# Normalising between the stages of a three-block network: row sums with one-column matmuls and a spread, or already spread sums from a block of ones

## The chip, the cores and the metric

The kernel runs on one core of one Trainium2 chip. The metric is the device time of one execution in microseconds (us), lower is better. Three runs of the kernel before gave a median of 3197.14 us (3194.56 to 3199.7).

## The reference

The input is 256 tokens of 1024 features, float32. Three blocks of layers follow each other: feed-forward layers, a hybrid of a short convolution and attention, sparse attention, attention with forget gates, a convolution module with a LayerNorm, a mixture of eight experts, a pooled and block attention, a cross-attention and a convolved feed-forward layer. Almost every layer begins with the same step, a normalisation of each token by its own root mean square:

```python
def rms_norm(x, g):
    xf = x.astype(jnp.float32)
    y = xf * lax.rsqrt(jnp.mean(xf * xf, axis=-1, keepdims=True) + EPS)
    return (y * g.astype(jnp.float32)).astype(x.dtype)

def modulate(x, g, shift, scale):
    return rms_norm(x, g) * (1 + scale[:, None]) + shift[:, None]
```

The convolution module has a LayerNorm over 768 features: subtract the mean, divide by the root of the variance plus EPS, times a gain, plus an offset.

## The kernel before

The activations lie turned: features on the partitions, tokens along the free dimension. `X` is eight tiles of 128 features by 256 tokens; `T` is scratch of the same shape. A norm therefore has to sum over partitions and tiles, and its result, one number for each token, is needed on every partition. Each weight matrix comes in chunks of 128x2048 floats into `ring`; ScalarE rounds a chunk to `whi` (line 1869), VectorE takes the rest as `wlo` (line 2792), and TensorE multiplies with three matmuls for each product (`mm3`, line 541): upper by upper, upper by lower, lower by upper. `hh` and `hl` are the same two parts of the normalised activations.

Each engine has a class (`Pe`, `Act`, `Dve`, `Pool`, `Sp`) that writes its own program in order; engines meet only at semaphores, by `wait_ge`. What an engine does around a norm is thus set by the order in which its class writes it.

A stage ends with a down projection (`down_steps`, line 767): output tiles j = 0 to 7, two of them to a bank of PSUM. After each pair VectorE adds the result to `X` (`finish`, line 2925, two instructions for a pair), ScalarE squares the new tiles into `T` (`squares`, line 1899: 0 and 1, 2 and 3, 4 and 5 as one instruction of 512 columns each, 6 and 7 alone), and TensorE sums the squares (`stat_part`, line 597). The table `NEXT` (line 519) says which norm follows which stage. In the last step of the stage TensorE puts the sums of tiles 0 and 1 behind output tile 5, those of 2 and 3 behind tile 6, and those of 4 to 7 behind tile 7. A sum is a matmul whose stationary operand is half a tile of squares (128 tokens) and whose moving operand is one column of ones, so a tile takes two, and the result has tokens on partitions, 128x2.

The tail of a norm then runs: `root` (line 1912) takes the square root of the 128x2 on ScalarE into `st`, `rinv` (line 2807) the reciprocal on VectorE, `spread` (line 622) brings it to all partitions with two matmuls against the identity, 128x256 in PSUM, and `scale` (line 2833) multiplies every tile of `X` by its gain and by that. ScalarE copies each tile to `hh`, VectorE subtracts for `hl`, and the first matmuls of the next stage start when `hl` of tile 0 is there. TensorE meanwhile runs `heat(6)` (line 646), twelve matmuls on a constant tile whose result nobody reads.

Nine norms come from `NEXT`: `hy`, three of feed-forward layers of block 1, `nsa`, `n_ffn2`, `cv`, `moe` and `n_ffn3`; a tenth entry, `final`, has sums of its own. The norm `moba` follows the experts, and its eight tiles are summed in one go by `stat` (line 590). In the convolution layer (`conv_layer`, lines 1405 and 3582) the mean goes the same way (`spread("mean")`), then VectorE subtracts it, and the norm `cvln` sums six tiles of squares. Some norms inside the attention stages already take another way: `wide_sum` (line 614) with a stationary block of ones or pairs, `wide_root` (line 1925) and `wide_inv` (line 3398) over the whole spread tile; `mem3` is one of these.

In the prediction an "instruction pair" of TensorE is a load of weights and its matmul; a float32 matmul of the program is two such pairs.

## Time and profile before

| | |
|---|---|
| median of 3 runs | 3197.14 us |
| the profiled execution | 3200.52 us |
| its span, first to last instruction | 3198.4 us |
| TensorE (PE) busy | 3072.9 us, 96% |
| VectorE (DVE) busy | 2305.3 us, 72% |
| ScalarE (ACT) busy | 1698.1 us, 53% |
| mean granted TensorE clock | 0.967 of full |

The busy shares are averages over stages with different limits. The page also has a chain of waits: from the last instruction back, at each step to what released it. A timeline lists the instructions of one engine in order of time, equal neighbours merged; PEld is TensorE's loading of weights, PE its matmuls.

### The profile page before, as it was taken

Reading aid. Unit: us, or ns where it says so; the run is one execution under the profiler, and the core shown is the slowest. Engines: PE = TensorE matmul, PEld = TensorE weight load, DVE = VectorE, ACT = ScalarE, POOL = GpSimd, SP = SyncE. Lnnn points to the kernel's source line nnn. Section 1 sums busy time; section 2 is a strip of 40 time slices with the busy share of each in tenths; the row PEclk is TensorE's granted clock in tenths of the full one; section 3 lists DMA queues with packets and bytes.
Section 4 is the critical chain, followed back from the end, with each engine's and each line's share of the span. In section 5 each row is a group of like instructions: output and inputs, shape, how many; then the busy total and the mean of one; then the engine's idle time right before and its main releaser. Section 6 shows DMA issues by size and latency. Waiting matters only on the chain.

```text
span 3198.4 us, 48532 instructions
## 1 busy us (share of the span) xinstructions
PE 3072.9 (96%) x20796; PEld 2821.9 (88%) x20796; DVE 2305.3 (72%) x2588; ACT 1698.1 (53%) x1905; POOL 84.1 (3%) x163
## 2 busy tenths in 40 slices
PE   8999899999988999899979999999999999999999
PEld 6999799999988998899968888888888888899999
DVE  5786668788555556654585898898898888666575
ACT  4434343443534435443535777777777777545453
POOL 1010001011000000000000000000000000000000
PEclk8999999999989999999988999999999999999999
DMA  7785458678421653235412999999899899533353
GB/s 284 261 324 192 158 185 302 230 293 307 159 73 67 221 207 132 80 145 185 171 41 99 367 352 343 361 355 362 340 353 356 342 357 365 201 119 132 118 187 118
DMA packets 112317, 739.27 MB, mean 231 GB/s; under 512 B 12481, under 2 KB 12481, under 8 KB 32097
## 3 DMA queue, kind: packets, MB, share of 16 engines
q1 hardware_dynamic: 89424, 651.21, 54.3%
q0 software_dynamic: 22672, 84.91, 7.4%
q8 instruction: 166, 2.72, 0.3%
q14 instruction: 55, 0.44, 0.0%
HBM read 735.01 MB, written 1.05 MB: 230 GB/s over the span
## 4 chain that ended last, share of the span: by engine, by line
PE 77%; DVE 7%; ACT 3%; issue 1%; DMA 1%; DVEq 0%; ACTq 0%
PE ps L539 57%; PE ps L538 18%; PE ps L548 2%; DVE wlo L2792 2%; DVE AF L2771 2%; ACT whi L1869 1%; DMA ring<-in_w 1%; DVE att L2780 0%; DVE gf L2774 0%; DVE hl L2762 0%; DVE AF L2762 0%; ACT cv L1854 0%; DVE gs L2777 0%; DVE T L2762 0%; ACT L1854 0%
## 5 line engine op out<-in xcount | busy, mean ns | idle before, releaser
L2792 DVE TENSOR_TENSOR wlo<-ring,whi 128x2048 fp32r<-128x2048 f32 x620 | 1417.1, 2290 | 451.7 <-ACT whi L1869 450.7
L1869 ACT ACTIVATE whi<-ring 128x2048 fp32r<-128x2048 f32 x620 | 1185.3, 1914 | 365.5 <-issue 200.6
L539 PE MATMUL ps<-whi,AR 128*128 128x512 f32 (+1 forms) x2884 | 912.7, 392 | 3.1 <-DVE wlo L2792 2.8
L539 PE MATMUL ps<-hh,whi 128*128 128x256 f32 x2464 | 696.0, 282 | 3.6 <-DVE wlo L2792 3.2
L539 PE MATMUL ps<-hh,wlo 128*128 128x256 f32 x2464 | 688.5, 279 | 0.0
L539 PE MATMUL ps<-hl,whi 128*128 128x256 f32 x2464 | 688.3, 279 | 0.0
L539 PEld LDWEIGHTS ps<-whi,AR 128*128 128x128 f32 x2884 | 537.2, 188 | 119.0 <-DVE wlo L2792 3.5
L539 PE MATMUL ps<-wlo,AR 128*128 128x512 f32 (+1 forms) x1442 | 558.5, 387 | 0.0
L539 PEld LDWEIGHTS ps<-hh,whi 128*128 128x128 f32 x2464 | 462.8, 188 | 8.9 <-DVE wlo L2792 3.4
L539 PEld LDWEIGHTS ps<-hl,whi 128*128 128x128 f32 x2464 | 462.9, 188 | 1.2 <-issue 1.0
L539 PEld LDWEIGHTS ps<-hh,wlo 128*128 128x128 f32 x2464 | 462.5, 188 | 0.3
L538 PE MATMUL ps<-AR,whi 128*128 128x256 f32 x2112 | 380.8, 282 | 0.0
L538 PEld LDWEIGHTS ps<-AR,whi 128*128 128x128 f32 x2112 | 324.9, 189 | 0.0
L539 PEld LDWEIGHTS ps<-wlo,AR 128*128 128x128 f32 x1442 | 272.2, 189 | 58.9
L538 PE MATMUL ps<-AR,wlo 128*128 128x256 f32 x1056 | 296.8, 281 | 0.0
L1854 ACT ACTIVATE gs<-ps 128x256 f32<-128x256 f32 (+1 forms) x167 | 75.7, 453 | 274.2 <-PE ps L539 250.2
L538 PE MATMUL ps<-hh,whi 128*128 128x256 f32 x656 | 196.3, 299 | 10.3 <-DVE hl L2762 6.4
L538 PEld LDWEIGHTS ps<-AR,wlo 128*128 128x128 f32 x1056 | 199.7, 189 | 0.0
L538 PE MATMUL ps<-hl,whi 128*128 128x256 f32 x656 | 191.3, 292 | 0.0
L538 PE MATMUL ps<-hh,wlo 128*128 128x256 f32 x656 | 190.9, 291 | 0.0
L1854 ACT ACTIVATE cv<-ps,att 128x256 f32<-128x256 f32 (+1 forms) x144 | 60.5, 425 | 206.4 <-DVE att L2780 206.3
L1854 ACT ACTIVATE AR<-gf 128x512 fp32r<-128x512 f32 x66 | 41.7, 632 | 239.1 <-DVE gf L2762 239.1
(247 smaller groups left out, 3267.8 us busy)
## 6 DMA issues: line engine op xcount, KB each, us to landing
ring<-in_w SPq DMA_DIRECT2D x620, 1024.0 KB, 5.0
rring<-in_r POOLq DMA_DIRECT2D x135, 512.0 KB, 4.8
first<-in_r POOLq DMA_DIRECT2D x16, 512.0 KB, 15.1
AF<-in_mem POOLq DMA_DIRECT2D x2, 1024.0 KB, 7.6
X<-in_x POOLq DMA_DIRECT2D x1, 1024.0 KB, 15.1
AF<-in_cst POOLq DMA_DIRECT2D x1, 1024.0 KB, 5.4
y_out<-X SPq DMA_DIRECT2D x1, 1024.0 KB, 3.9
cst<-in_cst POOLq DMA_DIRECT2D x1, 672.5 KB, 16.3
```

The costliest lines, as they stand in the source:

```text
L538: return self.e.matmul(out, l, r, start=start, stop=stop, skip_group_check=True)
L539: return self.e.matmul(out, l, r, start=start, stop=stop)
L548: return self.e.transpose(out, in_, self.N.ident[0:n, 0:n])
L1854: self.e.activation(out, in_, f, **kw).then_inc(*self.up(*keys))
L1869: self.e.activation(N.whi[:, c % HB, :], N.ring[:, c % RING, :], ACT.Copy).then_inc(N.sem["hi"], 1)
L2771: self.e.scalar_tensor_tensor(out=out, in0=a, scalar=s, in1=b, op0=op0, op1=op1).then_inc(*self.up(*keys))
L2792: self.e.tensor_tensor(N.wlo[:, c % HB, :], N.ring[:, c % RING, :], N.whi[:, c % HB, :].bitcast(F32), ALU.subtract).then_inc(N.sem["lo"], 1)
```

## The change

For the nine norms of `NEXT` other than `final`, for `moba` and for `cvln`, the stationary operand becomes the block of ones (128x128) and the moving operand a whole tile of squares (256 columns), so the sum of a token stands on all partitions at once. ScalarE takes the root of the 128x256 into `xbc`, VectorE its reciprocal in place, and `scale` reads `xbc`; `spread`, `root` and `rinv` go. TensorE's `heat` stands right behind the sums and has 16 matmuls where it had 12 (`moe`, which had none, gets 12). In the nine, VectorE first adds the squares of tiles 0 to 3 (`four_squares`, three instructions written between output tiles 5 and 6 in `finish`), and TensorE has no sums between the output tiles: it sums the added tile and tiles 4 to 7, behind tile 7. The mean of the convolution layer is summed with the block of ones too, and VectorE subtracts it straight from the sums by a scalar_tensor_tensor.

```diff
+WIDE = set(NEXT.values()) - {"final"} | {"moba", "cvln"}
...
     def stat_part(self, key, tiles, part, inds=None):
         n, b = len(tiles), self.ps((key, "ss"))
         for k in part:
             self.wait_ge("act", (key, "sq", k))
+            if key in WIDE:
+                i = self.mm(b[:, 0:S], self.N.ones[:, :], tiles[k], k == 0, k == n - 1)
+                continue
             for tb in range(2):
...
     def norm(self, key, X, which, n=8, T=None):
         T = self.N.T if T is None else T
-        if key not in self.row:
+        if key not in self.summed:
             self.stat(key, [T[:, k, :] for k in range(n)])
-        self.spread(key)
-        self.heat(6)
+        self.w4 += 1
+        self.heat(8)
         self.fresh = key
...
             if f == nf - 1 and key in NEXT:
                 if j == 5:
-                    self.take_row(NEXT[key])
-                    self.take((NEXT[key], "ss"))
-                    self.stat_part(NEXT[key], tiles, (0, 1))
-                elif j == 6:
-                    self.stat_part(NEXT[key], tiles, (2, 3))
+                    self.sum_place(NEXT[key])
+                if NEXT[key] == "final" and j in (5, 6):
+                    self.stat_part(NEXT[key], tiles, (2 * j - 10, 2 * j - 9))
             if j in cuts:
                 yield
         self.chunk_done()
         if f == nf - 1 and key in NEXT:
+            if NEXT[key] != "final":
+                self.wait_ge("dve", (NEXT[key], "four"))
+                self.stat_part(NEXT[key], tiles, (0,))
             self.stat_part(NEXT[key], tiles, range(4, 8))
...
-        self.take_row("mean")
         b = self.take(("mean", "ss"))
         for k, j in enumerate(CONV_ORDER):
             self.wait_ge(*(("dve", ("cv", "conv", j)) if j < 4 else ("act", ("cv", "conv", j))))
-            for tb in range(2):
-                t = self.mm(b[:, tb:tb + 1], N.c_acc[:, j, tb * P:(tb + 1) * P], N.ones[:, 0:1], k == 0 and tb == 0, k == 5,
-                            skip=True)
+            t = self.mm(b[:, 0:S], N.ones[:, :], N.c_acc[:, j, :], k == 0, k == 5)
         t.then_inc(*self.up(("mean", "ss")))
-        self.spread("mean", ready=("act", "sqrt"))
+        self.w4 += 1
...
         self.stat("cvln", [N.T[:, j, :] for j in range(6)])
-        self.spread("cvln")
-        self.heat(6)
+        self.w4 += 1
+        self.heat(8)
...
-        self.spread("moe")
+        self.heat(6)
...
         self.squares(key, X, n, ready or self.ready_x, T)
-        self.root(key, n * P)
+        self.wide_root(key, n * P, N.xbc[:, :])
...
     def norm(self, key, X, which, n=8):
-        self.rinv(key)
+        self.wide_inv(key, self.N.xbc[:, :])
         self.scale(key, X, which, n)
...
+            if j == 5 and NEXT.get(key, "final") != "final":
+                self.four_squares(NEXT[key])
+
+    def four_squares(self, key):
+
+        T = self.N.T
+        for k in (0, 2):
+            self.wait_ge("act", (key, "sq", k + 1))
+            self.tt(T[:, k, :], T[:, k, :], T[:, k + 1, :], ALU.add)
+        self.wait_ge("dve", self.here())
+        self.tt(T[:, 0, :], T[:, 0, :], T[:, 2, :], ALU.add, (key, "four"))
...
-            self.tt(N.c_acc[:, j, :], N.c_acc[:, j, :], b, ALU.subtract, ("cv", "d", j),
-                    *([("free", ("mean", "bc"))] if j == 5 else []))
-        self.rinv("cvln")
-        self.wait_ge("mm", ("cvln", "bc"))
-        b = self.ps(("cvln", "bc"))[:, 0:S]
+            self.stt(N.c_acc[:, j, :], b, -1.0 / 768, N.c_acc[:, j, :], ALU.mult, ALU.add, ("cv", "d", j),
+                     *([("free", ("mean", "ss"))] if j == 5 else []))
+        self.wide_inv("cvln", N.xbc[:, :])
+        self.wait_ge("dve", ("cvln", "inv"))
+        b = N.xbc[:, :]
...
-        self.rinv("moe")
-        self.scaled_rows("moe", N.T, N.X, N.V("norm_ffn_2", 1), 8, lambda k: ("moe", "z", k))
+        self.wide_inv("moe", N.xbc[:, :])
+        self.wait_ge("dve", ("moe", "inv"))
+        for k in range(8):
+            self.stt(N.T[:, k, :], N.X[:, k, :], N.V("norm_ffn_2", 1)[:, k:k + 1], N.xbc[:, :], ALU.mult, ALU.mult,
+                     ("moe", "z", k))
```

## Rows read from the trace of the kernel before

**Rows 1.** The page, part 4: the chain that ended last, by engine.
```profile
PE 77%; DVE 7%; ACT 3%; issue 1%; DMA 1%; DVEq 0%; ACTq 0%
```

**Rows 2.** Timeline, TensorE's weight loads, 611 to 622: start, us, engine, line, count.
```profile
611.98 0.97 PEld L538 LDWEIGHTS ps<-ones,T 128*128 128x128 f32 x8
...
618.90 2.54 PEld L539 LDWEIGHTS ps<-warm 128*128 128x128 f32 x12
621.37 0.19 PEld L538 LDWEIGHTS ps<-hh,whi 128*128 128x128 f32 x1
```

**Rows 3.** Timeline, VectorE, the same norm, 612 to 621.
```profile
612.25 0.88 DVE L2771 SCALAR_TENSOR_TENSOR X<-ps,mod,X 128x256 f32<-128x256 f32 x2 [0.57 <-PE ps L538]
...
619.36 1.26 DVE L2771 SCALAR_TENSOR_TENSOR T<-X,gain,ps 128x256 f32<-128x256 f32 x3 [1.32 <-PE ps L539]
620.54 0.48 DVE L2771 SCALAR_TENSOR_TENSOR hl<-T,mod,hh 128x256 fp32r<-128x256 f32 x1
```

**Rows 4.** Timeline, ScalarE, the same norm: the root.
```profile
617.58 0.26 ACT L1854 ACTIVATE st<-ps,cst 128x2 f32<-128x2 f32 x1 [0.75 <-PE ps L538]
```

**Rows 5.** Timelines of TensorE's loads, ScalarE, VectorE, 2849 to 2858: the norm mem3.
```profile
2849.90 3.32 PEld L539 LDWEIGHTS ps<-AF,ones 128*128 128x128 f32 x16
...
2853.67 0.47 ACT L1854 ACTIVATE xbc<-ps,cst 128x256 f32<-128x256 f32 x1 [2.86 <-PE ps L539]
...
2854.24 1.75 DVE L2777 RECIPROCAL xbc<-xbc 128x256 f32<-128x256 f32 x1 [2.71 <-ACT xbc L1854]
2856.05 2.29 DVE L2792 TENSOR_TENSOR wlo<-ring,whi 128x2048 fp32r<-128x2048 f32 x1
```

**Rows 6.** Timelines, VectorE: the norms hy and of the last feed-forward layer of block 1.
```profile
272.85 0.88 DVE L2771 SCALAR_TENSOR_TENSOR X<-ps,mod,X 128x256 f32<-128x256 f32 x2 [0.55 <-PE ps L538]
...
279.55 0.87 DVE L2771 SCALAR_TENSOR_TENSOR T<-X,gain,ps 128x256 f32<-128x256 f32 x2 [0.81 <-PE ps L539]
...
1009.21 0.87 DVE L2771 SCALAR_TENSOR_TENSOR X<-ps,mod,X 128x256 f32<-128x256 f32 x2 [0.54 <-PE ps L538]
...
1016.76 0.87 DVE L2771 SCALAR_TENSOR_TENSOR T<-X,gain,ps 128x256 f32<-128x256 f32 x2 [1.32 <-PE ps L539]
```

**Rows 7.** Timeline, TensorE's weight loads and VectorE, 405 to 421: after the hybrid stage.
```profile
409.30 1.53 PEld L538 LDWEIGHTS ps<-ones,T 128*128 128x128 f32 x8 [1.89 <-ACT T L1854]
...
407.66 2.44 DVE L2771 SCALAR_TENSOR_TENSOR X<-ps,mod,X 128x256 f32<-128x256 f32 x6
...
420.41 1.26 DVE L2771 SCALAR_TENSOR_TENSOR T<-X,gain,ps 128x256 f32<-128x256 f32 x3 [1.32 <-PE ps L539]
```

**Rows 8.** Timeline, VectorE: the norm n_ffn3.
```profile
2993.58 2.07 DVE L2762 TENSOR_TENSOR X<-X,ps 128x256 f32<-128x256 f32 x6
...
3004.91 0.87 DVE L2771 SCALAR_TENSOR_TENSOR T<-X,sm,ps 128x256 f32<-128x256 f32 x2 [1.32 <-PE ps L539]
```

**Rows 9.** Timelines, TensorE's weight loads and VectorE, 2744 to 2758: the norm moba.
```profile
2747.36 6.59 PEld L538 LDWEIGHTS ps<-ones,T 128*128 128x128 f32 x32 [3.22 <-issue]
...
2755.98 1.26 DVE L2771 SCALAR_TENSOR_TENSOR T<-X,sm,ps 128x256 f32<-128x256 f32 x3 [1.37 <-PE ps L539]
```

**Rows 10.** Timeline, TensorE's weight loads, 1673 to 1677: the mean, the next product.
```profile
1673.09 2.75 PEld L538 LDWEIGHTS ps<-ones,AF 128*128 128x128 f32 x24 [1.65 <-DVE hl L2762]
...
1676.99 0.33 PEld L538 LDWEIGHTS ps<-hh,whi 128*128 128x128 f32 x1
```

**Rows 11.** Busy time by stretch: us, PE, PEld, DVE, ACT, POOL, clock, DMA share, GB/s.
```profile
965.00:966.60 1.60, 0.00 (x0) 0.00 (x0) 1.60 (x3) 0.00 (x0) 0.00 (x0) 1.00 0.00 0
966.70:968.70 2.00, 2.00 (x16) 1.84 (x17) 0.98 (x3) 0.91 (x4) 0.00 (x0) 1.00 0.43 176
1018.90:1020.50 1.60, 1.60 (x9) 1.60 (x9) 1.60 (x5) 1.04 (x3) 0.00 (x0) 0.50 0.00 0
1301.20:1303.50 2.30, 0.00 (x0) 0.00 (x0) 2.30 (x4) 0.00 (x0) 0.00 (x0) 1.00 0.23 96
1304.00:1307.20 3.20, 3.20 (x15) 2.96 (x15) 1.65 (x5) 1.19 (x5) 0.00 (x0) 0.50 0.00 0
```

More of the change, by code:

```diff
@@ L418, in __init__ @@
         self.row, self.rt, self.base, self.span = {}, {}, 4, 4
+        self.summed = set()
         self.sq, self.sqs = 0, []
@@ L592, in stat, with sum_place @@
         n = len(tiles)
-        self.take_row(key)
+        self.sum_place(key)
+        self.stat_part(key, tiles, range(n), inds)
+    def sum_place(self, key):
+        self.summed.add(key)
+        if key not in WIDE:
+            self.take_row(key)
         self.take((key, "ss"))
-        self.stat_part(key, tiles, range(n), inds)
     def stat_part(self, key, tiles, part, inds=None):
@@ L2472, in conv_layer @@
         self.to_T("cvT", 2, "cvo", 6)
-        self.root("mean", 768, func=ACT.Copy)
         self.wait_ge("mm", "cv_mean")
         self.squares("cvln", N.c_acc, 6, lambda k: self.wait_ge("dve", ("cv", "d", k)), N.T)
-        self.root("cvln", 768)
+        self.wide_root("cvln", 768, N.xbc[:, :])
         for j in range(6):
@@ L2490, in moe @@
         self.wait_ge("act", f)
-        self.root("moe", 1024)
+        self.wide_root("moe", 1024, N.xbc[:, :])
         self.raws += 1
@@ L2837, in scale @@
             self.wait_ge("dve", ("part", which[1], 3 * which[2] + 1))
-        self.wait_ge("mm", (key, "bc"))
-        b = self.ps((key, "bc"))[:, 0:S]
+        if key in WIDE:
+            self.wait_ge("dve", (key, "inv"))
+            b = N.xbc[:, :]
+        else:
+            self.wait_ge("mm", (key, "bc"))
+            b = self.ps((key, "bc"))[:, 0:S]
         for k in range(n + 2):
@@ L2842, in scale @@
                 self.stt(N.T[:, k, :], X[:, k, :], gain[:, k:k + 1], b, ALU.mult, ALU.mult, (key, "n", k),
-                         *([("free", (key, "bc"))] if k == n - 1 else []))
+                         *([("free", (key, "bc"))] if k == n - 1 and key not in WIDE else []))
             if k >= 2:
@@ L3650, in conv_layer @@
         self.to_T("cvT", 2, "cvo", 6)
-        self.take_row("mean")
-        self.wait_ge("mm", ("mean", "bc"))
-        b = self.ps(("mean", "bc"))[:, 0:S]
+        self.wait_ge("mm", ("mean", "ss"))
+        b = self.ps(("mean", "ss"))[:, 0:S]
         for j in range(6):
             self.wait_ge(*(("dve", ("cv", "conv", j)) if j < 4 else ("act", ("cv", "conv", j))))
-            self.tt(N.c_acc[:, j, :], N.c_acc[:, j, :], b, ALU.subtract, ("cv", "d", j),
-                    *([("free", ("mean", "bc"))] if j == 5 else []))
-        self.rinv("cvln")
-        self.wait_ge("mm", ("cvln", "bc"))
-        b = self.ps(("cvln", "bc"))[:, 0:S]
+            self.stt(N.c_acc[:, j, :], b, -1.0 / 768, N.c_acc[:, j, :], ALU.mult, ALU.add, ("cv", "d", j),
+                     *([("free", ("mean", "ss"))] if j == 5 else []))
+        self.wide_inv("cvln", N.xbc[:, :])
+        self.wait_ge("dve", ("cvln", "inv"))
+        b = N.xbc[:, :]
         for j in range(8):
@@ L3664, in conv_layer @@
                 self.stt(N.c_acc[:, j, :], N.c_acc[:, j, :], N.V("conv_ln_g_2", 0)[:, j:j + 1], b, ALU.mult, ALU.mult,
-                         ("cvln", "n", j), *([("free", ("cvln", "bc"))] if j == 5 else []))
+                         ("cvln", "n", j))
             if j >= 2:
```

## The prediction

> **What bounds the kernel.** The chain of waits comes first: 77% of it is TensorE [rows 1], so a gain has to be time in which TensorE neither stands nor does avoidable work. Then the timelines around the norms, engine by engine, between the end of one stage and the first product of the next, because there the engines wait for each other in turn and nothing else covers the wait. In one such norm VectorE updates tiles 4 and 5 of `X` at 612.25 and starts scaling at 619.36, and the next stage's first product is loaded at 621.37 [rows 2, 3]. I count each norm from "tile 5 done" (612.25 + 0.88 = 613.13), which the change doesn't touch, to "scaling starts": 6.2 us here. The weight splits for the next chunks are done ahead, so an earlier start of scaling is an earlier stage, whatever bounds the stage later.
>
> **The sum on TensorE.** Before, eight instruction pairs of one column take 0.97 us, 0.12 us each, almost all of it weight loading [rows 2]. Sixteen of them stand between output tiles 5, 6 and 7 and sixteen behind tile 7. The change takes the first sixteen out: 1.9 us at full clock. Behind tile 7 it has five float32 matmuls of 256 columns, ten pairs. The nearest row is exact: in `mem3` sixteen such pairs begin at 2849.90 and occupy 3.32 us, the root starts at 2853.67 [rows 5]. So a pair is about 0.21 us (3.32 less one load of 0.19, over 15), and ten pairs lead from the first load to the root in 3.77 - 6 x 0.21 = 2.5 us.
>
> **The adds on VectorE.** Three tensor_tensor of 128x256 float32. Six such in a row take 2.07 us [rows 8]: 0.42 alone, 0.33 apart. The squares they need come off ScalarE pair by pair behind the updates, and in the timelines those of tiles 2 and 3 end before tile 5 is updated, or within 0.1 us of it. They start at 613.05, 613.39 and, because the third waits for the second, 613.85, and end at 614.27. Queued behind them are the updates of tiles 6 and 7, whose product without the sums is ready about 1.4 us after tile 5's: they start 0.6 us later than they could, but still earlier than now. Their squares are ready before TensorE reaches them. So the sums start at 614.3, 1.2 us after tile 5.
>
> **The tail.** Now from root to scaling: 619.36 - 617.58 = 1.8 us with `spread` inside [rows 3, 4]; at full clock VectorE waits 0.81 us for the spread instead of 1.32, 0.5 less [rows 3, 6]. After: root 0.47, reciprocal of 128x256 1.75, next instruction at 2856.05: 2856.05 - 2853.67 = 2.4 us [rows 5]. The tail gets 0.6 us longer at the clock of that norm, 1.1 at full clock. This is the cost of the change, eleven times. The Trainium skill ("VectorE: DVE Perf Modes", First, the fixed hardware budget) says that reciprocal is an iterated divide with a repeat count of 8; 8 x 256 / 0.96 GHz would be 2.1 us, an estimate, and eleven norms would then cost 4 us more than I take. The row with 1.75 us at this very shape decides.
>
> **Six norms at the end of stages where VectorE was free.** After: 1.2 + 2.5 + 2.4 = 6.1, with less rounding 6.0 us from tile 5 to scaling. Before: from 279.55 - 273.73 = 5.8 to 1016.76 - 1010.08 = 6.7 [rows 6], 6.2 in rows 3, mean of the six 6.3. Together -1.8 us: here the shorter stream and the longer tail nearly cancel.
>
> **Three norms where VectorE came late** (after the hybrid, `moe`, `n_ffn3`). VectorE was splitting the last chunk (2.29 us, as in rows 5) until 407.7 while the products were made, and TensorE, in front of output tile 6, stood 1.89 us for the squares of tiles 0 and 1, then ran at half clock [rows 7]. The change moves that wait behind tile 7, so output tiles 6 and 7 no longer wait. From tile 5 (407.66 + 2.44 = 410.10) to scaling it was 10.3 us, in `n_ffn3` 3004.91 - 2995.65 = 9.3 [rows 7, 8], `moe` between them with 9.9 in the same view; after 6.0: -4.3, -3.9, -3.3, together -11.5 at full clock. At half clock ten pairs take 2.1 us more each time, -5.2. There is now an idle stretch of about 2.4 us before the sums (tile 7's product at 408.9, added squares at 411.3), so either is possible; I take the middle, -8.4.
>
> **moba.** 32 pairs of one column, 6.59 us, 8.6 to scaling [rows 9]. After, sixteen pairs: 3.8 + 2.4 = 6.2, or 9.3 all at half clock: -2.4 to +0.7, I take -0.9.
>
> **Mean and cvln.** 24 pairs and a spread, next product at 1676.99 [rows 10]; after, twelve pairs of 0.21 us and no spread before the product: 1673.09 + 2.5 = 1675.6, -1.4. VectorE's subtraction is hidden by the 48 pairs of that product. Sums of cvln -0.1, tail +0.6. Together -0.9.
>
> **Heat.** It used to end at 621.44, while `hl` of tile 0 was there at 621.02: TensorE started 0.35 us late [rows 2, 3]. Now the sixteen follow the sums at once (done by about 618.7, or 620.2 at half clock) and hold up nothing: -0.35 in the five feed-forward norms, where TensorE is the slower one from there; in the others VectorE's scaling sets the pace, and I take nothing. Together -1.7. `moe`'s twelve fit in the 2.9 us before its first scaled tile.
>
> **The clock after the tail.** Heat ends, and TensorE idles some 2.2 to 2.7 us till the first product. How that is answered is open: after 2.0 us of idling at 965 the clock stayed 1.00, after 2.4 at 1301 the next 3.2 us were at 0.50 [rows 11]. The bound: 3.2 us of products at half clock cost 1.6 us, in five feed-forward norms 8. But now, too, some start at half clock (1018.9 to 1020.5) [rows 11], by my count of the granted clock 2.4 us over the five. Bounds -2.4 and +5.6. With half of the norms hit, 4 - 2.4 = +1.6; I take +1.2.
>
> **The sum.** -1.8 - 8.4 - 0.9 - 0.9 - 1.7 + 1.2 = -12.5 us. On the profiled span: 3198.4 - 12.5 = 3185.9. The profiled execution took 3200.52, 2.1 more than its span, and stands 3.4 over the median of the runs; the difference of 12.5 taken from the median gives 3184.6. Launch and end stay as they are. DMA is not asked for more.
>
> **Rivals.**
> 1. The clock holds everywhere: -1.8 - 11.5 - 2.4 - 0.9 - 1.7 - 2.4 = -20.7, 3176. For it: now one column at a time keeps the engine occupied at half clock (32 loads in 6.59 us, 0.21 each, against 0.12 [rows 2, 9]), and the change puts 256 columns there. Against it: the two idle stretches. Chance 0.18. The Trainium skill ("TensorE: Matmul & The Clock Gate", Part 1) has the rule on this side: the clock follows how busy the array has been lately, and half clock is what it has at rest. The trace agrees as far as rows 9 and 11 go; by the rule without regard to the idle stretches the time would be that of this rival.
> 2. The tail gives the gain back: every first product after a tail at half clock (+5.6), the three late norms' sums too (-5.2), moba +0.7: -1.8 - 5.2 + 0.7 - 0.9 - 1.7 + 5.6 = -3.3, 3194. For it: 2.4 us of idling at 1301. Chance 0.23.
> 3. Slower: the pause in front of the sums, 0.9 us in the six free norms, is enough to drop the clock there, after which ten pairs cost 2.1 us more in each. -3.3 + 6 x 2.1 = +9.3, 3206. It decides from two of the six on that rival 2 turns into no change. Against it: with one-column work in the same place the clock in those norms fell only around the root, not before tile 7 was done. Chance 0.05.
> 4. The change doesn't do what it says: the adds end later than tile 7's product by so much (squares 2 and 3 behind the table load on ScalarE) that the sums start as late as now. Then the three late norms keep the end of the wait, and only 1.7 + 0.9 are won, with +0.6 to +1.1 lost in each of eleven tails: about +6 with the clock as it is, 3203. ScalarE's squares were in time in the trace, chance 0.02.
>
> My forecast has 0.52. Faster by over 0.2% (about what a measurement of this kernel can tell from no change, 6.4 us, under 3190.7): the forecast nearly whole (0.50), rival 1, and a little of rival 2 (0.03): 0.71. Within 0.2%: 0.22. Slower: 0.07. The range: from rival 1 up to a little beyond rival 2, 3176 to 3197.
>
> **What would show it.** In the changed profile: no one-column loads between output tiles 5, 6 and 7 except for `final`; three VectorE adds of 0.42 us after tile 5 in nine norms; ten float32 pairs, 2.5 us from first load to root; root 0.47, reciprocal 1.75 in eleven places; from tile 5 to scaling 6.0 us in the six and, at full clock, in the three. Half-clock stretches at 409 and 2997 gone would speak for rival 1, new ones right at each first product for rival 2, half clock during the sums for rival 3. Wrong it would be if TensorE waited for the adds much longer than 1 us in the six, or if an earlier start of a stage met a chunk that isn't split.

## The result and the profile after

Beside five runs of the kernel before (median 3199.7 us) the changed kernel took 3181.33 us (3178.3 to 3181.96, five runs): a ratio of 0.9941, 95% interval 0.9925 to 0.9956, 18.9 us less. The time of the forecast, 3184.6, was close, 3.3 us off, and that is in part luck: beside the changed kernel the kernel before had a median 2.6 us above the one that the forecast started from. The difference was further off: -12.5 us is a ratio of 0.9961, outside the interval, and rival 1 with -20.7 us (0.9935) lies inside. The profiled execution took 3178.3 us, its span 3176.5.

The page of the changed kernel, the span, part 1 and the engines of part 4, answering to the table and [rows 1]:

```profile
span 3176.5 us, 48095 instructions
...
PE 3033.6 (96%) x20562; PEld 2777.6 (87%) x20562; DVE 2332.9 (73%) x2615; ACT 1700.9 (54%) x1904; POOL 84.6 (3%) x163
...
PE 76%; DVE 9%; ACT 2%; issue 1%; DMA 0%; DVEq 0%; ACTq 0%
```

TensorE is busy 39.3 us less (3072.9 before), VectorE 27.6 us more: eleven reciprocals of 1.75 us (19.3) and nine times three adds in 1.21 us (10.9), less eleven small reciprocals of 0.17 us and some trifles. The chain still runs on TensorE.

One of the six norms where VectorE is free, the counterpart of [rows 2] to [rows 4]. Changed kernel, timelines, TensorE's weight loads, VectorE, ScalarE (start, us, engine, line, operation, count, and in brackets the idle time before):

```profile
605.83 2.02 PEld L543 LDWEIGHTS ps<-T,ones 128*128 128x128 f32 x10 [0.88 <-DVE T L2771]
607.88 2.08 PEld L543 LDWEIGHTS ps<-warm 128*128 128x128 f32 x16
612.38 0.19 PEld L542 LDWEIGHTS ps<-hh,whi 128*128 128x128 f32 x1 [2.42 <-issue]
```

```profile
603.77 0.88 DVE L2780 SCALAR_TENSOR_TENSOR X<-ps,mod,X 128x256 f32<-128x256 f32 x2 [0.55 <-PE ps L542]
604.57 1.21 DVE L2771 TENSOR_TENSOR T<-T 128x256 f32<-128x256 f32 x3
605.69 0.87 DVE L2780 SCALAR_TENSOR_TENSOR X<-ps,mod,X 128x256 f32<-128x256 f32 x2
608.80 1.75 DVE L2786 RECIPROCAL xbc<-xbc 128x256 f32<-128x256 f32 x1 [2.24 <-ACT xbc L1864]
610.59 1.28 DVE L2780 SCALAR_TENSOR_TENSOR T<-X,gain,xbc 128x256 f32<-128x256 f32 x3
```

```profile
608.29 0.47 ACT L1864 ACTIVATE xbc<-ps,cst 128x256 f32<-128x256 f32 x1 [1.28 <-PE ps L543]
```

Four numbers are to be read from these rows. The pause before the sums is 0.88 us (0.9 foretold), ten pairs lead from 605.83 to the root in 2.46 us (2.5), root to scaling is 610.59 - 608.29 = 2.30 us (2.4), and tile 5 done (603.77 + 0.88 = 604.65) to scaling is 5.94 us (6.0).

One of the three norms where VectorE came late, the counterpart of [rows 7]. Changed kernel, timeline, weight loads, then VectorE:

```profile
407.98 2.02 PEld L543 LDWEIGHTS ps<-T,ones 128*128 128x128 f32 x10 [2.47 <-DVE T L2771]
410.03 2.07 PEld L543 LDWEIGHTS ps<-warm 128*128 128x128 f32 x16
414.53 0.19 PEld L542 LDWEIGHTS ps<-hh,whi 128*128 128x128 f32 x1 [2.43 <-issue]
```

```profile
405.54 1.26 DVE L2780 SCALAR_TENSOR_TENSOR X<-ps,mod,X 128x256 f32<-128x256 f32 x3
406.72 1.21 DVE L2771 TENSOR_TENSOR T<-T 128x256 f32<-128x256 f32 x3
407.84 0.87 DVE L2780 SCALAR_TENSOR_TENSOR X<-ps,mod,X 128x256 f32<-128x256 f32 x2
...
412.74 1.28 DVE L2780 SCALAR_TENSOR_TENSOR T<-X,gain,xbc 128x256 f32<-128x256 f32 x3
```

The 1.89 us wait in front of output tile 6 is now a wait of 2.47 us behind tile 7, and the sums behind it run at 0.20 us a pair: full clock. Tile 5 done (405.54 + 1.26 = 406.80) to scaling (412.74) is 5.94 us where it was 10.3.

Where the clock went, changed kernel, busy time by stretch (columns as in [rows 11]): the first products after the hybrid stage and of the norm shown above, those of `hy` and `n_ffn3`, and the sums of `moe`:

```profile
414.60:418.60 4.00, 4.00 (x34) 4.00 (x35) 4.00 (x11) 2.55 (x5) 0.00 (x0) 1.00 0.02 4
612.40:616.40 4.00, 3.99 (x34) 4.00 (x35) 4.00 (x11) 2.57 (x6) 0.00 (x0) 1.00 0.01 4
...
279.90:283.30 3.40, 3.40 (x18) 3.40 (x18) 3.40 (x10) 2.22 (x5) 0.00 (x0) 0.50 0.02 5
1696.40:1699.80 3.40, 3.39 (x8) 2.76 (x9) 0.62 (x2) 0.75 (x2) 0.00 (x0) 0.51 0.28 116
2983.30:2986.70 3.40, 3.40 (x19) 3.40 (x18) 3.40 (x10) 2.03 (x5) 0.00 (x0) 0.50 0.00 0
```

After the same pause of 2.4 us some first products run at 2.4 GHz and some at 1.2. Over the whole span the mean granted clock is 0.978, before 0.967. The time at half clock, summed from the trace's clock records, is 208 us before and 142 after. 50 of these 66 us lie inside the nine norms (53 before, 3.6 after), whose lengths the table below has, and 13 in the stages between them.

**Where the time went.** I cut both spans at the same marks: from "tile 5 done" to the next stage's first product (nine norms), the same for `final`, from the first sum to the first product for `moba`, and all that lies between, "the stages". Times in us, for the profiled executions of some kernels that are told of below; the last column is the time at half clock within the stages:

| | nine norms | final | moba | stages | span | clock | half clock in stages |
|---|---|---|---|---|---|---|---|
| before | 84.0 | 7.9 | 10.7 | 3095.8 | 3198.4 | 0.967 | 142.5 |
| changed | 70.1 | 9.2 | 9.5 | 3087.7 | 3176.5 | 0.978 | 129.3 |
| changed, once more | 69.3 | 7.5 | 9.5 | 3094.0 | 3180.4 | 0.977 | 141.5 |
| late one-column sums (1) | 64.8 | 7.8 | 11.0 | 3104.6 | 3188.3 | 0.969 | 156.0 |
| the same with adds (3) | 65.1 | 8.4 | 11.0 | 3102.1 | 3186.6 | 0.969 | 155.4 |
| mean, cvln and moba alone (5) | 77.9 | 8.0 | 9.5 | 3102.5 | 3197.9 | 0.969 | 156.4 |
| changed, no heat (7) | 69.3 | 8.5 | 9.5 | 3096.9 | 3184.2 | 0.972 | 158.5 |
| reciprocal root, no adds (8) | 53.1 | 8.3 | 7.7 | 3086.2 | 3155.3 | 0.979 | 127.6 |

The nine norms give 14 to 15 us against this one profile of the kernel before, and `moba` 1.2. The stages between give 8.1 us in one execution and 1.8 in another of the same kernel, so 6 of the 8 are chance; what stays in both is the convolution stage, 2.7 to 3.5 us shorter. The kernel before has one profile only. Experiment 5 has the same program in its nine stage ends, and there they take 77.9 us instead of 84.0 and the stages 3102.5 instead of 3095.8, so each column is good to 6 us or so.

The last column shows what moves the stages. Take half of the time at half clock from the length of the stages, and all fourteen profiles of this study come out between 3018 and 3027 us, although the lengths themselves spread from 3084 to 3105. In the stages a microsecond at half clock costs about half a microsecond, and the rest of their work stays the same. One caution: the execution profiled without heat was the fastest of its twelve, 9 us under their median, so its row flatters that kernel.

### The profile page after: what moved, and what is told of

The parts are those of the page before. It is cut to its first block, busy times and chain, and to the rows that moved or that the text cites. A ratio compares the mean times of both kernels' runs of the same rounds, so it can differ in the third digit from the quotient of the medians.

```text
span 3176.5 us, 48095 instructions
## 1 busy us (share of the span) xinstructions
PE 3033.6 (96%) x20562; PEld 2777.6 (87%) x20562; DVE 2332.9 (73%) x2615; ACT 1700.9 (54%) x1904; POOL 84.6 (3%) x163
## 4 chain that ended last, share of the span: by engine, by line
PE 76%; DVE 9%; ACT 2%; issue 1%; DMA 0%; DVEq 0%; ACTq 0%
PE ps L543 58%; PE ps L542 16%; PE ps L552 2%; DVE wlo L2801 2%; DVE AF L2780 2%; ACT whi L1879 1%; DVE xbc L2786 1%; DVE T L2771 1%; DVE T L2780 0%; DVE att L2789 0%; DVE hl L2771 0%; DVE gf L2783 0%; DVE AF L2771 0%; ACT cv L1864 0%; DVE gs L2786 0%
```

## The experiments

Ratios are to the kernel before on the same chip, with 95% intervals; 0.001 is 3.2 us.

**1. Only the order.** From the kernel before, the sums of tiles 0 to 3 are moved behind output tile 7. Nothing else changes.

```diff
-                    self.stat_part(NEXT[key], tiles, (0, 1))
-                elif j == 6:
-                    self.stat_part(NEXT[key], tiles, (2, 3))
+                if NEXT[key] == "final" and j in (5, 6):
+                    self.stat_part(NEXT[key], tiles, (2 * j - 10, 2 * j - 9))
...
+            if NEXT[key] != "final":
+                self.stat_part(NEXT[key], tiles, range(4))
             self.stat_part(NEXT[key], tiles, range(4, 8))
```

> The kernel before with one edit: in the nine stage ends the one-column sums of tiles 0 to 3, which stood between output tiles 5, 6 and 7, stand behind tile 7 with the others. No adds on VectorE, no block of ones, spread and 12 heat matmuls as before. Theory 1 (most of the gain is the wait for squares in front of output tile 6, in the three stage ends where VectorE is late): about 3 us each in these three and 0.2 to 0.3 in the six others, 9 to 11 us faster than before. Rival (the gain comes from the wide sums, the adds and what they do to the clock): within 3 us of before. In the profile: from tile 5 to scaling 5.8 to 6.3 us in all nine by theory 1, 9 to 10 in the three by the rival.

Measured: 0.9971 (0.9959 to 0.9983), 3190.71 us: 9.3 us less, half of the whole gain, from a step that takes no instruction away, as theory 1 had it. After the hybrid stage, the timelines of this kernel, weight loads and VectorE:

```profile
413.05 3.82 PEld L538 LDWEIGHTS ps<-ones,T 128*128 128x128 f32 x32 [0.49 <-ACT T L1855]
417.51 0.93 PEld L539 LDWEIGHTS ps<-cst,st 128*128 128x128 f32 x4 [0.64 <-DVE st L2778]
418.32 2.68 PEld L539 LDWEIGHTS ps<-warm 128*128 128x128 f32 x12
420.88 0.33 PEld L538 LDWEIGHTS ps<-hh,whi 128*128 128x128 f32 x1
```

```profile
411.41 3.22 DVE L2772 SCALAR_TENSOR_TENSOR X<-ps,mod,X 128x256 f32<-128x256 f32 x8
...
418.78 1.26 DVE L2772 SCALAR_TENSOR_TENSOR T<-X,gain,ps 128x256 f32<-128x256 f32 x3 [1.32 <-PE ps L539]
```

The products of tiles 6 and 7 are done before VectorE comes, so it updates its last eight tiles in one stretch; the wait in front of tile 6 is gone. Tile 5 to scaling falls from 10.3, 9.9 and 9.3 us in the three late norms to 4.9, 5.1 and 4.5, which is shorter than the changed kernel's and than the 5.8 to 6.3 foretold. But the spread's four loads take 0.93 us, against 0.52 at full clock (below), and the next product starts at half clock.

**2. The whole change without the adds.** TensorE sums all eight tiles behind tile 7, sixteen pairs.

```diff
-                self.wait_ge("dve", (NEXT[key], "four"))
-                self.stat_part(NEXT[key], tiles, (0,))
+                self.stat_part(NEXT[key], tiles, range(4))
...
-            if j == 5 and NEXT.get(key, "final") != "final":
-                self.four_squares(NEXT[key])
```

> The changed kernel without the three adds on VectorE: the block of ones is multiplied with all eight tiles of squares behind tile 7. Six more float32 pairs of 0.21 us (1.3 us), but the sums can start 0.9 us earlier. Theory (adds are worth what they save TensorE): root 0.4 us later in each of nine norms, 3 to 4 us slower than the changed kernel, 15 us faster than before. Rival (the 0.9 us pause in front of the sums costs clock): as fast as the changed kernel or up to 4 us faster, with fewer stretches at half clock.

Measured: 0.9936 (0.9923 to 0.995), 3180.24 us; the changed kernel on the same chip 0.9941. Timeline, weight loads:

```profile
606.68 3.33 PEld L543 LDWEIGHTS ps<-T,ones 128*128 128x128 f32 x16
610.03 2.08 PEld L543 LDWEIGHTS ps<-warm 128*128 128x128 f32 x16
```

The sums take 1.3 us longer and start without the pause of 0.9, as VectorE's updates aren't put off. From tile 5 to scaling it is 6.3 to 6.5 us in the free norms (5.9 to 6.0 with the adds), 5.3 to 5.6 in the three late ones (5.9 to 7.7). The adds cost what they save, and the theory that they are worth 3 to 4 us falls. The sign of the rival is there: half clock within 12 us of the first products of eight norms (the nine without `moe`) sums to 3.2 us, against 13.4 and 16.5 in the two profiles of the changed kernel. That the missing pause is the cause isn't shown, as the sums are longer too.

**3. The order and the adds, one-column sums.** Experiment 1 with `four_squares` and its wait, the tail as before.

> The kernel before with the adds and the sums behind tile 7, but the one-column matmuls, root and reciprocal of 128x2 and spread kept (mean, cvln and moba as before). Twenty pairs of 0.12 us are as long as ten of 0.21; the tail is 0.6 us shorter than the changed kernel's at half clock and 1.1 at full clock. Theory (the wide tail is a cost of the change): from tile 5 to scaling 5.0 to 5.6 us instead of 5.94, so as fast as the changed kernel although mean, cvln and moba are not changed: 14 to 20 us faster than before. Rival (one-column sums let the clock fall, and the wide ones hold it): about 8 to 12 us faster than before, with a half-clock stretch in each tail.

Measured: 0.9958 (0.9944 to 0.9971), 3187.87 us: 13.4 us less by the ratio and 12.1 by the medians, between the two ranges and nearer the rival's, whose half-clock stretch is there in each of the nine tails. Timelines of this kernel at the norm shown first, weight loads and VectorE:

```profile
611.68 2.31 PEld L538 LDWEIGHTS ps<-ones,T 128*128 128x128 f32 x20 [0.88 <-DVE T L2764]
614.63 0.52 PEld L539 LDWEIGHTS ps<-cst,st 128*128 128x128 f32 x4 [0.64 <-DVE st L2779]
615.07 2.15 PEld L539 LDWEIGHTS ps<-warm 128*128 128x128 f32 x12
617.15 0.29 PEld L538 LDWEIGHTS ps<-hh,whi 128*128 128x128 f32 x1
```

```profile
609.63 0.88 DVE L2773 SCALAR_TENSOR_TENSOR X<-ps,mod,X 128x256 f32<-128x256 f32 x2 [0.54 <-PE ps L538]
...
615.38 1.26 DVE L2773 SCALAR_TENSOR_TENSOR T<-X,gain,ps 128x256 f32<-128x256 f32 x3 [0.80 <-PE ps L539]
```

Tile 5 (610.51) to scaling is 4.87 us, 1.07 less than in the changed kernel: the price of the wide tail at full clock, 1.1 by the prediction. Over the nine norms this kernel is 5.0 us shorter than the changed one and still 5.6 us slower by the medians on this chip (3187.87 against 3182.23): its stages are 8 to 14 us longer, at a granted clock of 0.969, with 14 to 26 us more at half clock in them, which makes 7 to 13. So where it stands the wide form costs time, and what it gives comes by the clock of the stages; that was in no term of my sum. Two limits: 5.3 to 6.2 of the 8 to 14 us lie in the convolution stage, where this kernel also keeps the one-column mean and `cvln` (its mean runs at half clock, 5.6 us from first load to next product against 3.9 before), and the wide mean, `cvln` and `moba` are worth 3.5 us by experiment 5. (Both one-column kernels have the stages 6 to 9 us longer than the one profile of before, too, with 13 us more at half clock. Experiment 5, whose stage ends are those of before, has them as long, so this need not come from their edits.)

**4. The changed kernel once more,** beside experiments 1 to 3.

> The changed kernel again, beside the three others on the same chip: 16 to 21 us faster than before. Between two profiles of it the stretches at half clock outside the norms should differ by some; if the 1.8 us that the changed kernel had won before its first changed norm, and the 4 us in the experts' stage, are chance, they come out otherwise here.

Measured: 0.9941 (0.9927 to 0.9954), 3182.23 us. The free norms have 5.94 to 6.04 us again, while `moe` has 6.04 (7.73 in the first profile, where its sums fell to half clock) and the one after the hybrid stage 6.83. A time of one place is good to 1 us or so where the clock is in play.

**5. Mean, cvln and moba alone** in the new form, the nine norms as before (`WIDE = {"moba", "cvln"}`).

> The kernel before with only the parts outside the nine stage ends: mean, cvln and moba with the block of ones, wide root and reciprocal, heat of 16 behind the sums. The stage ends keep their one-column sums. Theory (my sum was too low here: the changed kernel needed 134 to 135 us from the first product of cv to tile 5 before moe, the kernels with the old form 138 to 140): 4 to 7 us faster than before, 3 to 5 of it between cv and moe. Rival (my prediction: -0.9 for mean and cvln, -0.9 for moba; the rest of those stretches is chance): 1 to 3 us faster.

Measured: 0.9989 (0.9976 to 1.0002), 3197.65 us, twelve runs: 3.5 us less, between 7.7 less and 0.6 more. By the marks `moba` gives 1.2 and the convolution stage 1.1. The interval of the time holds both my new theory (4 to 7 us) and the prediction's 1.8; the marks, 2.3 together, speak for the prediction.

**6. More heat.** 28 matmuls behind the sums instead of 16, so that TensorE doesn't idle before the first product.

```diff
-        self.heat(8)
+        self.heat(14)
```

> The changed kernel with 28 heat matmuls behind the sums instead of 16 (ten norms and cvln; moe keeps its 12). They end before the first product of the next stage at full clock. Theory (the idle stretch behind the heat drops the clock, and the first products pay up to 1.6 us): no half-clock stretch at the first products, 2 to 6 us faster than the changed kernel, 20 to 25 us faster than before. Rival (the clock there falls for what went before, or costs nothing because VectorE paces): within 2 us of the changed kernel.

Measured: 0.9953 (0.9939 to 0.9966), 3184.64 us. In its profile no first product of the nine norms other than `moe`'s had a half-clock stretch within 12 us (13.4 us in the changed kernel, 16.5 in the other execution), and the profiled execution was its fastest, 3175.06. The other five lie between 3182 and 3190, with clocks of 0.976 and 0.977 where the profiled one had 0.980. So more heat can clear the half clock at the first products, but the median gains nothing that can be measured. Whether the slower runs had it cleared too isn't known, as they have no trace.

**7. No heat.** The changed kernel with the sixteen heat matmuls taken out of nine norms and `cvln`. Those of `moe` and `final` stay.

```diff
-        self.w4 += 1
-        self.heat(8)
+        self.w4 += 2
```

> The changed kernel with no heat matmuls behind the sums (ten norms and cvln; moe keeps its 12). Theory (the clock at the first products hangs on what TensorE does in the tail): a half-clock stretch at nearly every first product, up to 1.6 us each in five feed-forward norms and less in the others, 4 to 9 us slower than the changed kernel, so 10 to 14 us faster than before. Rival: heat is worth nothing here, within 2 us of the changed kernel.

Measured: 0.9984 (0.9972 to 0.9996), 3195.04 us, twelve runs: without heat three quarters of the gain are lost, (0.9984 - 0.9941) x 3200 = 14 us. Weight loads of this kernel after the hybrid stage, and the busy time by stretch there:

```profile
409.39 2.02 PEld L543 LDWEIGHTS ps<-T,ones 128*128 128x128 f32 x10 [2.46 <-DVE T L2769]
415.94 0.29 PEld L542 LDWEIGHTS ps<-hh,whi 128*128 128x128 f32 x1 [4.53 <-issue]
```

```profile
416.00:420.00 4.00, 4.00 (x19) 4.00 (x20) 4.00 (x11) 2.54 (x5) 0.00 (x0) 0.50 0.00 0
```

The tail is as long as ever (tile 5 to first product 69.3 us over the nine), but TensorE idles 4.5 us and makes 19 matmuls in the next 4 us where the changed kernel makes 34. Half clock within 12 us of the same eight first products sums to 33.5 us. The theory is right in kind and its 4 to 9 us are too small.

**8. Root and reciprocal in one step.** The reciprocal on VectorE goes; ScalarE's function for the reciprocal root writes `xbc` straight from the sums, in eleven norms. No adds (as in experiment 2).

```diff
+        if key in WIDE:
+            self.act(out, self.ps((key, "ss"))[:, 0:out.shape[-1]], ACT.Abs_reciprocal_sqrt, (key, "inv"), ("free", (key, "ss")),
+                     scale=1.0 / div, bias=self.N.C("eps"))
+            return
...
-        self.wide_inv(key, self.N.xbc[:, :])
...
-            self.wait_ge("dve", (key, "inv"))
+            self.wait_ge("act", (key, "inv"))
```

> The changed kernel without the adds, and in the eleven norms ScalarE's function for the reciprocal root takes the place of root and reciprocal, so the tail is one instruction of about 0.47 us on ScalarE and none on VectorE (less exact than the two steps). Theory (the tail lies on the path in full): 1.75 us and one hop less in each of eleven norms, 19 to 21 us faster than the kernel without adds, about 38 to 42 us faster than before. Rival (a shorter tail runs into something else: tables of ScalarE, the heat of 1.9 us, chunks that are not split): less than 12 us faster than the kernel without adds.

Measured: 0.9857 (0.984 to 0.9873), 3155.67 us: 45.8 us less than before by the ratio, 25 less than experiment 2, where 19 to 21 were expected. With experiment 9 it is the fastest kernel of the study. How much less exact its results are than those of the two steps was not measured. Timelines, weight loads, ScalarE and VectorE:

```profile
605.84 3.32 PEld L543 LDWEIGHTS ps<-T,ones 128*128 128x128 f32 x16
609.19 2.08 PEld L543 LDWEIGHTS ps<-warm 128*128 128x128 f32 x16
611.90 0.19 PEld L542 LDWEIGHTS ps<-hh,whi 128*128 128x128 f32 x1 [0.63 <-issue]
```

```profile
609.60 0.48 ACT L1863 ACTIVATE xbc<-ps,cst 128x256 f32<-128x256 f32 x1 [2.13 <-PE ps L543]
```

```profile
610.11 1.27 DVE L2783 SCALAR_TENSOR_TENSOR T<-X,gain,xbc 128x256 f32<-128x256 f32 x3 [3.09 <-ACT xbc L1863]
```

Root to scaling is 0.51 us instead of 2.30: 1.79 us, eleven times 19.7, of which the marks show 16.1 in the nine norms (against experiment 2's 69.2) and 1.8 in `moba`. The tail lies wholly on the path. The 5 us beyond it are not traced to a place; the stages have 10 us less at half clock than in experiment 2. The pause before the first product is 0.63 us instead of 2.4, and the clock is 0.979 to 0.982 in its runs.

**9. The same with the adds.**

> The kernel with the one-step root and, again, the three adds on VectorE. Theory (adds are worth nothing: they save TensorE 1.3 us of sums but make it wait 0.9 us and idle): within 3 us of the kernel with the one-step root, about 1.3 to 1.5% faster than before. Rival (adds are worth their 0.3 us in each of nine norms and more): 3 to 6 us faster than without.

Measured: 0.9865 (0.9845 to 0.9885), 3157.08 us. As between experiment 2 and the changed kernel, the adds make no difference that can be measured.

**10. The one-step root without heat.**

> The kernel with the one-step root, without adds and without the 16 heat matmuls behind the sums. TensorE then idles 2.6 us in each tail instead of 0.7. Theory (what TensorE does in the tail sets the clock of the first products): half clock at most first products, 5 to 14 us slower than with heat, 0.9 to 1.3% faster than before. Rival (a tail as short as this needs no heat): within 3 us of the kernel with heat.

Measured: 0.9913 (0.9897 to 0.9929), 3170.59 us, clock 0.971 to 0.976. Heat is worth 18 us by the ratios here (15 by the medians), with TensorE idle for only 2.7 us without it (4.5 in experiment 7). Seven of the eight first products have half clock right behind them, 23.7 us together, none with heat. The 5 to 14 us of the theory were too small again.

**11. Heat later.** The changed kernel, its sixteen heat matmuls held back until ScalarE's root is done.

```diff
         self.w4 += 1
+        self.wait_ge("act", (key, "sqrt"))
         self.heat(8)
```

> The changed kernel with the 16 heat matmuls waiting for the root, so TensorE idles about 0.8 us before and 1.6 us behind them instead of 2.5 us behind them. The same work, the same path. Theory (one long idle stretch next to the first products drops the clock in about half of the norms): no or one half-clock stretch at the first products, 2 to 5 us faster than the changed kernel (0.65 to 0.75% faster than before). Rival (where the heat stands doesn't matter, only that it is there): within 1.5 us of the changed kernel.

Measured: 0.9939 (0.9921 to 0.9957), 3182.81 us, clocks of 0.976 to 0.981. The half clock at the same eight first products falls from 13.4 us to 1.0 in its profile, and the time stays. In the stages as a whole the time at half clock is 136 us, between the 129.3 and 141.5 of the changed kernel's two profiles, so as much of it turned up in other places. Runs of this kernel differ by 12 us among themselves, with the clock, and the interval doesn't part the theory from its rival.

**12. Four heat matmuls in the gap, one-column sums.** Experiment 3, with four matmuls on the constant tile between the sums and the spread, twelve behind it as before.

```diff
-        self.spread(key)
-        self.heat(6)
+        b = self.take(("heat", self.heats))
+        self.heats += 1
+        self.warmth(b, 4)
+        self.spread(key)
+        self.warmth(b, 12)
```

> The third kernel (one-column sums of the added tile and tiles 4 to 7, root, reciprocal and spread as before) with four more heat matmuls in the 0.64 us between the sums and the spread, in all the norms that have heat; the twelve behind the spread stay. The changed kernel had a granted clock of 0.977 with wide sums and heat, 0.969 with wide sums and no heat, and the one-column kernels with twelve heat matmuls 0.967 to 0.969. Theory (the one-column sums, some 2.3 to 3.8 us of TensorE with hardly a column in them, are what lets the clock fall; some heat behind them does not make up for it): clock 0.968 to 0.970, ratio 0.995 to 0.997 to the kernel before, like the third kernel (0.9958). Rival (it is the number and the nearness of the heat matmuls, the kind of sums does not matter): clock 0.975 to 0.978 and some 10 us faster than the third kernel, ratio about 0.992 to 0.993.

Measured: 0.9946 (0.9925 to 0.9967), 3185.71 us, clocks of 0.968 to 0.971. Weight loads of this kernel at the last feed-forward norm of block 1:

```profile
1005.11 2.31 PEld L538 LDWEIGHTS ps<-ones,T 128*128 128x128 f32 x20 [0.89 <-DVE T L2775]
1007.34 0.83 PEld L539 LDWEIGHTS ps<-warm 128*128 128x128 f32 x4
1008.06 0.96 PEld L539 LDWEIGHTS ps<-cst,st 128*128 128x128 f32 x4
1008.90 2.39 PEld L539 LDWEIGHTS ps<-warm 128*128 128x128 f32 x12
```

TensorE has no pause left between sums and first product, and yet behind the twenty loads of one-column sums the four heat loads take 0.83 us and the spread 0.96. In the norm shown first they take 0.54 and 0.52, full clock, so it doesn't happen every time; in the other eight of the nine norms there are 1.7 to 6.9 us at half clock between tile 5 and the first product. The clock stays with the one-column kernels, against the rival that only number and nearness of the heat matter. The time doesn't separate the two: its interval holds both experiment 3's ratio and the changed kernel's.

## Why the prediction came out as it did

**The steps that held.** No sums between the output tiles; three adds (0.4 us apart, 1.2 us together) that put off the updates of tiles 6 and 7; sums 1.2 us after tile 5 (605.83 - 604.65 = 1.18); 5.94 us to scaling in five of the six free norms and 6.04 in `cv`, together -2.0 us against -1.8. The tail is 2.30 us, not 2.4, and experiment 3 puts its price at 1.1 us. The Trainium skill ("VectorE: DVE Perf Modes", First, the fixed hardware budget) gives reciprocal a repeat count of 8, an estimate of 2.1 us here; the eleven reciprocals of 1.75 us speak against it.

**The three late norms.** -4.4, -2.2 and -3.3 us, -9.9 against the middle of -8.4 that I took (-10.7 in the second profile). Two are at the full-clock end; in `moe` the sums ran at half clock for a while (rows above, 0.51). Experiment 1 shows the cause alone: the order, not the wide form, brings it. How much there was to win varies by itself: in experiment 5 the same three, unchanged, take 6.1, 8.8 and 8.2 us where before had 10.3, 9.9 and 9.3.

**Heat and the late start.** First product after scaling: 1.79 us in place of up to 2.11, over the nine -2.0 with rounding, against -1.7.

**moba, mean and cvln.** `moba` -1.2 (-0.9; its upper bound of +0.7 should have been +1.0, as sixteen pairs at half clock cost 3.4 us more at my 2.1 for ten). From the mean's first load to the next product 2.5 us, as foretold (3.9 before). The convolution stage is 2.7 to 3.5 us shorter, experiment 5 has 1.1 of them alone; I had 0.9.

**What was mis-sized.** The clock term, +1.2 with bounds of -2.4 and +5.6, asked what the pause of 2.4 us would do to the first products of five feed-forward norms. Counted in the same way, half of the time at half clock there, it measured +0.9 and +2.7 us in the two profiles: so far it held. What it left out is the clock in the rest of the stages. I had argued for rival 1 that one-column work keeps the clock low, and then gave this a price in the norms alone and none in the stages. The sum beside the two profiles, as differences from the profile of before:

| term, us | forecast | changed | once more |
|---|---|---|---|
| six free norms to scaling | -1.8 | -2.0 | -2.0 |
| three late norms | -8.4 | -9.9 | -10.7 |
| scaling to first product | -1.7 | -2.0 | -2.0 |
| moba | -0.9 | -1.2 | -1.2 |
| convolution stage | -0.9 | -3.5 | -2.7 |
| first products at half clock | +1.2 | +0.9 | +2.7 |
| `final` | 0 | +1.3 | -0.4 |
| rest of the stages | 0 | -5.4 | -1.7 |
| span | -12.5 | -21.9 | -18.0 |

The convolution stage has 2 to 9 us less at half clock, and the rest of the stages moves with it too. With one profile of the kernel before, these last rows can't be told from chance. The experiments show the clock's part better, in pairs, all runs of a kind together:

| sums | heat | granted clock |
|---|---|---|
| one-column, also between the last tiles (before) | 12 | 0.964 to 0.971 |
| one-column (experiments 1, 3, 12) | 12 or 16 | 0.966 to 0.971 |
| wide (experiment 7) | none | 0.966 to 0.973 |
| wide (changed, experiments 2, 6, 11) | 16 or 28 | 0.974 to 0.981 |
| wide, one-step root, none (10) | none | 0.971 to 0.976 |
| wide, one-step root (8, 9) | 16 | 0.978 to 0.982 |

Wide sums without heat hardly raise the clock with the two-step tail (with the one-step root, where TensorE idles less, they raise it some), and heat beside one-column sums doesn't; the two together do. The time at half clock in the stages says the same without the norms' own share: 142.5 to 156.4 us in the five profiles with one-column sums in the nine norms, 153.2 and 158.5 in the two with wide sums and no heat, 119.2 to 141.5 in the seven with both. Heat is worth 14 us in the wide form (experiment 7 against the changed kernel). What the wide form is worth through the clock, with heat in both, no run has by itself: experiment 3 is 5.6 us slower than the changed kernel, of which experiment 5 gives 3.5, with a wide interval, to the mean, `cvln` and `moba`.

So the forecast had the mechanism right at the places it looked at, and 6.4 us too little: 1.5 to 2.3 us in the late norms, about 2 in the convolution stage, and the rest in stages that it took as untouched, where the clock decides.

**The rivals.** Rival 1 came closest in time and half in mechanism: the stretches at 409 and 2997 are gone, as it asked, but five first products, `moba`'s among them, still fall to half clock, as rival 2 asked. Rival 1's -2.4 for those products did not come. The Trainium skill ("TensorE: Matmul & The Clock Gate", Part 1) was named with it, for the rule that the clock follows how busy the array has been lately: experiment 7 agrees with it (clock 0.966 to 0.973 without heat), and the five first products show that the idle stretch could not be left out. Rival 3 (half clock in the sums of the free norms) and rival 4 (late adds) did not happen: pause 0.88 us and sums at 0.20 us a pair in the free norms.

**What stays open.** Why a stage that no edit touches has more or less time at half clock from kernel to kernel and from run to run, and why a full clock at the first product (experiments 6 and 11) leaves the median where it was. How much of the 18.9 us the clock gave: the kernel before has no second profile. One-column sums with heat of the wide kernel's size directly behind could not be placed, as the spread stands in between.

## What to carry to other kernels

Time the tail of a reduction that all engines wait for as a chain of single instructions, and ask of each whether another function or engine makes it unnecessary: here one step of 0.5 us in place of 2.3 us gave more (25 us in eleven places, at a cost in exactness that no run here shows) than the whole change. A wait that TensorE meets in the middle of its last products belongs behind them, which costs no instruction and gave half of this gain. Before pricing a shorter form of work on TensorE, ask what it does to the granted clock in the whole span: a form that is 1 us shorter in place (experiment 3) came out 5.6 us longer in all, with more time at half clock in the stages.

## What the runs showed of the hardware that I had not expected

ScalarE's reciprocal root of a 128x256 from PSUM takes 0.48 us, the same as its square root (0.47); with it the ScalarE-then-VectorE pair of 2.30 us is one step of 0.51.

One-column float32 sums went with a fallen clock although TensorE was occupied: twenty pairs in 2.31 us were followed, with no pause, by heat at half clock in one norm of experiment 12 (0.83 us for four loads), while sixteen heat matmuls behind ten wide ones took 2.08 us, full clock, in each norm of the changed kernel whose rows are shown here.

Filling the idle time before a product with matmuls whose result nobody reads is worth 14 to 18 us of 3200 over ten places. The half clock right behind eight first products explains less than that: 17 to 20 us more of it without heat (33.5 against 13.4 and 16.5), so at most 10 us of time.

The length of the stages followed the clock almost alone: their time less half of the time at half clock was 3018 to 3027 us in fourteen profiles of kernels whose stages took 3084 to 3105 us.
